# Branch hints, early flag reads, a shorter one-hot sum and other loads in a fused diffusion block with a mixture of experts

## The reference, cut to what matters

```python
mod = silu(c) @ w_ada + b_ada            # six vectors of 1024: sh1, sc1, g1, sh2, sc2, g2
h = rmsnorm(x, norm1_g) * (1 + sc1) + sh1            # x: 2048 tokens of 1024
b, cg, xin, q, k, v, ga, gb = split(h @ w_in)
ya = (b * conv3(cg * xin)) @ w_a
yb = window_attention(rope(q), rope(k), v, k_ctx, v_ctx, sink) @ w_b
x = x + g1 * ((sigmoid(ga) * ya + sigmoid(gb) * yb) @ w_o)
h = rmsnorm(x, norm2_g) * (1 + sc2) + sh2
# top-1 of 4 groups, top-2 of its 8 experts: every token goes to two of 32 experts
for e in range(32):
    a, u = split(h @ w_up[e]); y += combine[:, e] * ((silu(a) * u) @ w_down[e])
out = rmsnorm(x + g2 * y, final_g)
```

## Time and profile before

| | us |
|---|---|
| median of 3 runs (lowest, highest) | 888.68 (887.53, 889.03) |
| profiled execution | 881.92 |
| span of its slowest core, core 1 | 880.2 |
| spans of the eight cores | 851.8 to 880.2 |

### The profile page before, as it was taken

How to read it: one execution, slowest core, us unless ns; L and a number is a source line. 1 busy time by engine, 2 the same in 40 slices (tenths; PEclk the granted TensorE clock), 3 DMA queues, 4 the chain that set the end, 5 groups by cost and what they waited for, 6 DMA issues and landing times.

```text
span 880.2 us, 14399 instructions; the slowest of 8 cores (851.8 to 880.2 us)
## 1 busy us (share of the span) xinstructions
PE 773.6 (88%) x5578; PEld 431.1 (49%) x5578; DVE 523.6 (59%) x1116; ACT 397.6 (45%) x719; POOL 254.5 (29%) x329
## 2 busy tenths in 40 slices
PE   5989999995999999999999947799888868889694
PEld 1345554452455444454445425566665646557341
DVE  0468766895653666468789785756433433434177
ACT  2255544673666765434263251243344343334453
POOL 2022020000011211211311115466676665552200
PEclk9998999998999999999999975799999998999898
DMA  8999999999999999999799998689999999994596
GB/s 146 210 223 187 193 143 152 149 152 149 143 127 104 204 176 135 198 155 176 160 142 141 133 191 157 135 231 209 259 257 265 266 249 265 241 279 185 175 350 240
DMA packets 37008, 168.42 MB, mean 191 GB/s; under 512 B 11700, under 2 KB 13876, under 8 KB 28611
## 3 DMA queue, kind: packets, MB, share of 16 engines
q0 software_dynamic: 28864, 146.65, 86.4%
q1 hardware_dynamic: 8068, 20.77, 7.1%
HBM read 234.26 MB, written 58.72 MB: 333 GB/s over the span
## 4 chain that ended last, share of the span: by engine, by line
PE 64%; DMA 18%; DVE 9%; ACT 3%; issue 3%; another core or an unknown queue 1%; POOL 0%; SPq 0%; POOLq 0%; DVEq 0%; ACTq 0%
PE ps L587 59%; DMA sb<-wex 7%; DMA sb<-wad 4%; DMA sb<-x 4%; DVE sb L605 2%; PE ps L940 2%; PE ps L1432 2%; ACT sb L600 2%; DVE sb L617 2%; DMA wbf<-wex 2%; DVE sb L620 1%; DMA sb<-ng 1%; DVE sb L1451 1%; ACT sb L602 1%
## 5 line engine op out<-in xcount | busy, mean ns | idle before, releaser
L587 PE MATMUL ps<-sb 128*128 128x512 bf16 (+10 forms) x4536 | 706.8, 310 | 82.8 <-DVE sb L620 16.0
L587 PEld LDWEIGHTS ps<-sb 128*128 128x128 bf16 (+4 forms) x4536 | 369.9, 102 | 392.5 <-issue 102.5
L600 ACT ACTIVATE sb<-ps 128x512 bf16<-128x512 f32 (+4 forms) x390 | 215.6, 594 | 293.3 <-PE ps L587 197.9
L605 DVE TENSOR_TENSOR sb<-ps,sb 128x256 bf16<-128x256 f32 (+4 forms) x196 | 85.7, 447 | 181.3 <-PE ps L587 92.3
L600 ACT ACTIVATE sb<-ps,sb 128x512 bf16<-128x512 f32 x136 | 86.0, 688 | 60.9 <-PE ps L587 47.6
L1420 POOL DMA_INDIRECT sb<-hd,sb x68 | 77.2, 1136 | 76.5 <-PE ps L587 29.5
L671 POOL DMA_DIRECT2D wbf<-wex x72 | 35.8, 499 | 191.0 <-DMA wbf<-wex 174.1
L617 DVE SCALAR_TENSOR_TENSOR sb<-sb 128x1024 f32<-128x1024 f32 (+5 forms) x93 | 84.1, 913 | 4.0 <-ACT sb L899 2.5
L1496 POOL DMA_INDIRECT yd<-sb x66 | 72.3, 1096 | 48.8 <-ACT sb L600 27.7
L605 DVE TENSOR_TENSOR sb<-sb 128x512 bf16<-128x512 f32 (+6 forms) x113 | 81.2, 724 | 5.2 <-ACT sb L602 3.5
L602 ACT ACTIVATE sb<-sb 128x1024 bf16<-128x1024 f32 x45 | 47.5, 1056 | 72.3 <-DVE sb L605 40.7
(11 more groups left out here) (59 smaller groups left out, 251.4 us busy)
## 6 DMA issues: line engine op xcount, KB each, us to landing
wbf<-wex POOLq DMA_DIRECT2D x72, 384.0 KB, 12.5
sb<-wbf POOLq DMA_DIRECT2D x18, 1536.0 KB
sb<-wex POOLq DMA_DIRECT2D x16, 1536.0 KB
sb<-x POOLq DMA_DIRECT2D x26, 512.0 KB, 14.0
sb<-wad POOLq DMA_DIRECT2D x12, 1024.0 KB, 25.5
sb<-wsl POOLq DMA_DIRECT2D x8, 1024.0 KB, 36.4
sb<-yd SPq DMA_DIRECT2D x16, 512.0 KB, 11.4
out<-sb SPq DMA_DIRECT2D x16, 512.0 KB, 3.1
```

Source lines behind the costliest of these rows:

```text
L587: ins = e.matmul(o, lhsT=l, rhs=r, start=s0, stop=s1)
L600: S.op("act", lambda e: e.activation(out=out, in_=in_, func=func, scale=scale), reads=[in_] + list(extra), writes=w)
L605: S.op(eng, lambda e: e.tensor_tensor(out=out, in0=a, in1=b, op=op), reads=[a, b], writes=[out])
```

## The change

Six things are changed together. (1) The join goes; each engine that enters the region waits at the end of each of its parts for everything in the region. The flag is read 24 (PE), 40 (ACT, DVE) or 12 (POOL) operations ahead of the branch, a hint location is marked there, and the branch becomes a compare-and-branch that carries the hint. (2) The rows of the last item are placed by one-hot products for the first three groups (six tiles) alone; for the other five groups they are scattered into `yd` after the second-choice loads of the first three groups have landed, and the second-choice loads of those five groups wait for that scatter. (3) `wide` holds six tiles instead of five. (4) `C2` and `S2` are no longer loaded: a constant of [128, 192] is loaded by SP at the start, and POOL adds a row part and a column part for each table. (5) Modulation blocks 0 to 3 have four buffers, the two of before and weight slots 4 and 5; their loads are written five steps ahead of their products, blocks 4 and 5 use the first two buffers again, and the gate weights of slots 4 and 5 now follow the products of blocks 2 and 3. (6) `G2b` is made before the last routing steps, by the same products in the banks 6 and 7.

```diff
@@ order @@
-        cuts, join = self.region
+        cuts = self.region
...
-            if i != join and any(lo <= k < hi for k in d):
-                ops[i]["deps"] = set(k for k in d if not lo <= k < hi) | {join}
-        ops[join]["deps"] = set(k for k in ops[join]["deps"] if not lo <= k < hi)
+            ops[i]["deps"] = set(k for k in ops[i]["deps"] if not lo <= k < hi)
@@ emit @@
-                    def emit_region(j):
-                        v_ = eng.value_load(self.flags[j], min_val=0, max_val=1)
-                        with eng.If(v_ > 0):
...
+                        def branch(j, v_, loc):
+                            eng.br_cmp(v_, 1, end, "over%d_%s" % (j, e), "IS_LT").branch_hint(loc)
+                        cut = max([len(parts[0]) - HINT_AHEAD[e]] + [i + 1 for i, wo in enumerate(parts[0]) if wo[1].get("flags")])
+                        emit_ops(parts[0][:cut])
+                        loc = eng.mark_branch_hint_location()
+                        v_ = flag(0)
+                        emit_ops(parts[0][cut:])
+                        branch(0, v_, loc)
+                        for j in range(nr):
+                            with nc_.body("over%d_%s" % (j, e), valid_engines=[eng.engine]):
+                                emit_ops(parts[j + 1])
                                 for k, v in rfinal[j]:
                                     eng.wait_ge(sems[k], v)
...
+HINT_AHEAD = dict(pe=24, act=40, dve=40, pool=12)
@@ build_program @@
+        cst = view(Z1 + 512, 192)
         sdma(ccs, cc_d, "c_cc")
+        sdma(cst, cs_d, "c_cs")
...
-        def late_loads():
-            gdma(C2, c2_d, "c_c2", [("xl", 5)]); gdma(S2, s2_d, "c_s2", [("xl", 5)])
+        for i, t_ in enumerate((C2, S2)):
+            r_ = cst[:, i * 96:i * 96 + 32].unsqueeze(2).to_broadcast([128, 32, 64]); c_ = cst[:, i * 96 + 32:i * 96 + 96].unsqueeze(1).to_broadcast([128, 32, 64])
+            o_ = t_.rearrange("p (r c) -> p r c", c=64)
+            S.op("pool", lambda e, o_=o_, r_=r_, c_=c_: e.tensor_tensor(out=o_, in0=r_, in1=c_, op=ALU.add), reads=[cst], writes=[t_], cost=4.6)
...
-        wsb = [wsx[0], wsx[1], view(P0 + 2048, 4096, BF16)]
+        wsb = [(wsx[0], ("wsx", 0)), (wsx[1], ("wsx", 1)), (slotf(4), ("w", 4)), (slotf(5), ("w", 5))]
+        wsb += wsb[0:2] + [(view(P0 + 2048, 4096, BF16), ("wsx", 2))] * 2
...
             if i % 4 == 1:
-                main.append((2.5, mod2_step(i // 4)))
+                main.append((0.0, lambda n=i // 4: mod2_load(n)))
+            if i % 4 == 2 and i >= 6:
+                main.append((2.5, mod2_step((i - 6) // 4, False)))
             if i % 4 == 3:
                 main.append((0.0, gate_load(i // 4)))
-        main += [(1.0, mod2_finish)]
+        main += [(2.5, mod2_step(5, False)), (1.0, mod2_finish)]
...
+        G2b = view(Q30 + 2048, 1024, BF16)
+        expand(mod2T[:, 24:32], G2b)
         for f_ in rs3:
             f_()
...
+                if i == NA - 4 and lo == 0:
+                    for e_ in ("pe", "act", "dve", "pool"):
+                        S.ops[S.op(e_, lambda e: e.nop(), reads=[eidi], writes=[("br", e_)], cost=0.05)]["flags"] = True
...
+        NPL = 3
...
-        for q, b in yord:
+        early_y = [(q, b) for q, b in yord if b == 0 or q < NPL]
+        for q, b in early_y:
...
-        join = S.op("pool", lambda e: e.nop(), writes=[("join", 0)], cost=0.05)
...
         Dn(NA - 1)
+        for s_ in range(2):
+            ix = rowi[0][:, s_, LE:LE + 1]
+            S.op("pool", lambda e, s_=s_, ix=ix: e.indirect_dma_start(
+                out=yd_d, out_offset=bass.IndirectOffsetOnAxis(ap=ix, axis=0),
+                in_=YLt[s_], in_offset=None, bounds_check=2 * L - 1, oob_is_err=False),
+                reads=[YLt[s_], ix, ("yz", s_)] + [("yl", q, 1) for q in range(NPL)], writes=[("yd", NA - 1, s_)], dma=("yz", s_), cost=0.8)
+        for q in range(NPL, 8):
+            yload(q, 1, "sp", ydk + [("yd", NA - 1, s_) for s_ in range(2)])
...
-        wide = (1, 4, 7, 10, 13)
+        wide = (7, 8, 10, 11, 13, 14)
...
+                lst = [(b_[:], identb, ya, True, False)] + xl + [(b_[:], identb, yb, False, q >= NPL)]
+                rd = [identb, identf, ya, yb] + ([xv] if xl else [])
+                if q < NPL:
+                    lst += [(b_[:], PL[s][:, q, k_, :], YLt[s][:, hs], False, s == 1) for s in range(2)]
```

More of the change, by code:

```diff
@@ L399, in emit_ops, with flag @@
                                 ins.then_inc(sems[k], 16 if k[1] == "d" else 1)
-                    def emit_region(j):
-                        v_ = eng.value_load(self.flags[j], min_val=0, max_val=1)
-                        with eng.If(v_ > 0):
-                            emit_ops(parts[j + 1])
-                            if e == "pool":
+                    nc_, end = eng.bass, "after_over_" + e
+                    if e == "sp":
+                        emit_ops(parts[0])
+                    else:
+                        def flag(j):
+                            return eng.value_load(self.flags[j], min_val=0, max_val=1)
+                        def branch(j, v_, loc):
[9 more added lines that the diff above has]
+                                emit_ops(parts[j + 1])
                                 for k, v in rfinal[j]:
                                     eng.wait_ge(sems[k], v)
[L407 to L411, removed]
+                                if j + 1 < nr:
+                                    branch(j + 1, flag(j + 1), eng.mark_branch_hint_location())
+                                else:
+                                    eng.br(end)
+                        nc_.switch_bb(end)
                     emit_ops(parts[-1])
@@ L840, in build_program @@
         v_step([16, 17])()
-        wsb = [wsx[0], wsx[1], view(P0 + 2048, 4096, BF16)]
+        wsb = [(wsx[0], ("wsx", 0)), (wsx[1], ("wsx", 1)), (slotf(4), ("w", 4)), (slotf(5), ("w", 5))]
+        wsb += wsb[0:2] + [(view(P0 + 2048, 4096, BF16), ("wsx", 2))] * 2
         def mod2_load(n):
-            i = n % 2 if n < 6 else 2
-            gdma(wsb[i], wad_d[4 + n], ("wsx", i))
+            w2, key = wsb[n]
+            gdma(w2, wad_d[4 + n], key)
         act(esb, esb, AF.Exp)
@@ L853, in gate_load, with mod2_step @@
             return lambda: gdma(slotf(i), src, ("w", i), [("xl", 17)])
-        def mod2_step(n):
+        def mod2_step(n, load=True):
             def f():
-                mod2_load(n)
-                w2 = wsb[n % 2 if n < 6 else 2]
+                if load:
+                    mod2_load(n)
+                w2 = wsb[n][0]
                 w_ = w2.rearrange("p (k n) -> p k n", n=512)
@@ L1567, in build_program @@
             i0 = i1
-        join = S.op("pool", lambda e: e.nop(), writes=[("join", 0)], cost=0.05)
-        S.region = (cuts, join)
+        S.region = cuts
         S.flags = [eidi[0:1, NDYN + k0:NDYN + k0 + 1] for k0 in KREG[:-1]]
@@ L1587, in sum_step @@
                 xl = [(q4(b_[:]), identf, xv, False, False)] if t in wide else []
[L1588 to L1590 removed]
+                lst = [(b_[:], identb, ya, True, False)] + xl + [(b_[:], identb, yb, False, q >= NPL)]
+                rd = [identb, identf, ya, yb] + ([xv] if xl else [])
+                if q < NPL:
+                    lst += [(b_[:], PL[s][:, q, k_, :], YLt[s][:, hs], False, s == 1) for s in range(2)]
+                    rd += [PL[s][:, q, k_, :] for s in range(2)] + [YLt[s][:, hs] for s in range(2)]
+                mm(b_[:], lst, rd)
                 if xl:
@@ L1648, in _host_consts @@
     pm[swm, m_] = 1.0
-    return np.ascontiguousarray(c2), np.ascontiguousarray(s2), ident, np.ascontiguousarray(m01), pm
+    byrow = (p % 32 < 16)[:, None]
+    rows = np.arange(32) * 64
+    cs = np.concatenate([f_ for t_ in (c2, s2) for f_ in (np.where(byrow, t_[:, rows], 0.0), np.where(byrow, 0.0, t_[:, 0:64]))], axis=1).astype(np.float32)
+    return np.ascontiguousarray(cs), ident, np.ascontiguousarray(m01), pm
 def _kslot(w, nk):
```

22 lines of the change are left out of this document (6 added, 16 removed).

## The result

The changed kernel takes 896.38 us in the median against 888.86 us of the kernel before: 1.0077 times as long, with a 95% interval of 1.0050 to 1.0105. The prediction was 875.6 us, faster with a chance of 0.85; direction and range were wrong. One of the four runs, at 955.23 us with one half of the chip at a lower clock, is left out of the ratio. The profiled execution took 895.66 us, the span of its slowest core, again core 1, is 893.9 us.

The account below looks back on a forecast made before the run. PE and the DMA engines were both taken as near their limits, PE's waits for particular transfers mattering. Terms 7.5 + 0 + 1.5 - 0.3 + 4.4 = 13.1 us gave 868.8 us profiled, 875.6 median; range near 866 to 886.

Parts of the forecast that it names:

- Modulation loads: PE's wait for modulation block 3: four buffers let its load leave earlier, gain 7.5 us, bounds 0 and 11.2.
- the modulation gain does not arrive: Rival, chance 0.20: earlier modulation loads make other transfers late, PE stands as long elsewhere before 600 us; 883.1 us.
- Rotary tables: Start: two table loads go, POOL's two additions fall in its idle time; taken as 0, bounds -0.9 and +2.
- the nearest rows: POOL's additions at the start: 2.0 us each from a POOL fill, 2.6 from a VectorE row; 4 us and more together.
- G2b: Between routing and first expert: its 5.5 us of products and copies move into PE gaps; gain 1.5 us, bounds 0 and 5.5.
- Flags, hints, join: Last branch: removing its stall gives 0 since sums wait for `yd`; early flag reads cost 0.3 us, bounds -0.7 and 0.
- The end: Final sums: fewer PE products against a new scatter-and-read round trip; gain 4.4 us, bounds 6.6 gain and 10.9 loss.
- T: Landing of `yload(3, 1)`, the read behind the last item's scatter at the end; taken as 847.4 us.
- the uncrowded rows: Round trip at the end: a 4.2 us scatter and 4.6 us read put the landing at 844.8 us.
- the crowded ones: Round trip at the end: medians of 15.7 us for scatters and 11.4 for `yd` reads put the landing at 863.1 us.
- The Trainium skill's rule: Round trip at the end: DMA engines alternate queues by packet, so the landing would be nearer 845 than 863 us.

Follow-up runs that it names:

- the repeats: Two follow-up kernels, one of them with only the new end (1.0047), with the instruction lists of the kernel before up to the last items.
- The runs with the gap: Kernel before with no expert-weight copies from the twentieth to the first residual `x` loads: 1.0385 with four modulation buffers, 1.0446 with modulation loads as before.
- the moved copies: Kernel before plus constant tables, `G2b` moved and eight expert-weight copies moved to the last gate stage in the program: 0.9957 with four modulation buffers, 0.9973 without.
- the spread folds: Kernel before plus constant tables, `G2b` moved and the eight `wo` folds spread among the last scores: 1.0027 with four modulation buffers, 1.0056 without.

## Why the prediction was wrong

**Modulation loads, predicted -7.5 us, measured +6.5 alone (4.4 to 8.7).** This is the step that failed most. The first half holds: the stall is gone, and at the middle of the scores PE is 7 to 14 us ahead in the pairs of kernels with and without the four buffers. The failed step is "the DMA share is 0.96 there, which leaves 0.04 x 234 = 9.4 us of room for the same transfers". The room was looked for behind 256 us; from 100 to 225 us the engines are at a share of 1.01 in the mean of the cores, also in the kernel before, and by 350 us they have worked for 346 us in the repeats. PE busy for 99% of the stage did not mean that nothing was nearly late: what PE needs next, `wo`, leaves no earlier and shares the engines with copies that nothing needs yet. When PE came 13.6 us early, VectorE waited for `wo`, and PE for VectorE. The runs with the gap show it: only with the copies away does the lead stay. So the rival "the modulation gain does not arrive", given 0.20, is what happened to the gain; a loss on top was not in it. That the four buffers cost 0.7% on top (1.0073 alone; 1.0077 with them against 1.0000 without) is measured but not explained. It is not there in every company: in the three pairs of which both were timed on the same chip, the moved copies (0.9957 with them, 0.9973 without), the spread folds (1.0027, 1.0056) and the gap (1.0385, 1.0446), they cost nothing. Of the changed kernel with and without them, the one with them had 40.6 MB instead of 41.2 MB at 250 us; from 200 to 225 us its engines moved 3.4 MB instead of 3.7 at the same share of 1.01, while the copies held half of their time instead of 0.29. Whether the loss comes from there stays open.

**Rotary tables, predicted 0 (-0.9 to +2), measured 1.8 us faster, not to be told from none.** The additions took 7.25 us together on core 1, above the 4 us of the nearest rows and inside POOL's idle time. The load's price was wrong: "0.3 us at 358 GB/s, 0.9 at 110" counts bytes, while its place ahead of a load of small packets cost the first product 7 us. That cost nothing that the time shows: the first stage ended 0.6 us later than in the repeats.

**G2b, predicted -1.5, measured -0.6 (-2.8 to +1.5).** Inside its interval, which holds no change as well.

**Flags, hints, join, predicted -0.3, measured +2.3 (0.5 to 4.0).** That the branch's stall is worth nothing was right. "Without the branch's stall the sums can still not start before 831.67: 0 by itself" overlooked the products at half clock directly ahead of the sums: with them the sums began at a granted 0.95, without them at 0.64, which is 1.3 us on the six cores. The rest of the 2.3 us stays open.

**The end, predicted -4.4, measured +4.2 alone (2.5 to 5.9).** From the issue of item 32's last scatter it was 48.6 us by the prediction and 59.7 on core 1. The landing T of `yload(3, 1)`: 24.6 predicted, 852.81 + 3.94 - 829.87 = 26.9 measured. The guess near the uncrowded rows was nearly right, against 40.3 by the crowded ones. The Trainium skill's rule weighed there ("DMA: Bandwidth & Descriptors", Queues, rings and completion order) put it near 22; the trace agrees in so far as 26.9 is nearer to that than to 40.3. PE from T to its end: 19.6 predicted, 876.50 + 5.30 - 856.80 = 25.0 measured, of which 2.34 is the wait for VectorE to free a bank; the rest is mostly half clock behind each gap (granted 0.68 and 0.66, the last number but two of these rows):

```profile
857.00:862.00 5.00, 5.00 (x13) 2.00 (x12) 2.63 (x7) 2.30 (x6) 0.00 (x0) 0.68 1.02 342
...
877.00:882.00 5.00, 4.79 (x11) 1.52 (x9) 2.33 (x7) 1.47 (x5) 0.00 (x0) 0.66 0.56 210
```

From PE's end to VectorE's: 3.9 predicted, 7.8 measured (889.57 - 881.80). This last is a slip in the sum: 3.9 was taken from the last tile's addition, while the rows of before had PE's end at 868.45 and VectorE's at 875.75, 7.3 apart. With 7.3 in its place and T as assumed, the end would have come out at a gain of 1 us instead of 4.4. So the terms that failed here are PE's time behind the round trip, priced at full clock and without a wait, and the tail of VectorE; with the one-hot sums for twelve tiles, where the gaps are gone, the loss is gone too.

The sum of the terms measured alone, 6.5 - 1.8 - 0.6 + 2.3 + 4.2 = 10.6 us, stands against 6.8 us (4.4 to 9.3) for the whole, each term with about 2 us of its own uncertainty. Taken back from the changed kernel, the modulation loads are worth 0.8% and the end 1.0%, more than the 0.5% of the end alone; these runs and those of the parts alone were timed on different chips.

## What to carry to other kernels

In this kernel PE and the DMA engines were both busy for 95% and more of a stage, and removing a stall of PE moved the wait to the next transfer. Ask which load the engine needs after the stall, whether the change makes it leave earlier, and what else the DMA engines carry at that time. Pulling other loads forward did not help; the two versions whose intervals lie below 1, both only just, had two MB of reads fewer and `G2b` moved, and others with both don't differ from before, so that the bytes are the reason is not shown. And a block of work that follows a wait must be priced at the clock that it finds: work that runs ahead of it may be part of its speed.

## What the runs showed of the hardware that was not expected

A load of 4 KB in 128 packets of 32 bytes took 2.5 us to land where its packets began at 2.3 us, before the 8 KB packets of another queue at 3.1 us, and 13.9 us where they began at 5.05 us, behind them. The same 148 records of PE took 36.78 us behind eight products at half clock and a gap of 0.59 us, and 38.28 us behind a gap of 3.30 us. And a background stream that looked as if it could be paused, since nothing reads what it writes before 560 us, cost 34 and 39 us when its pause left the engines idle for 32 and 40.
